# Two transformer blocks on one core: later convolutions in the projection stage, one product moved to GpSimd, and a new order of small steps

## The reference

```python
gu, gv, q, k, v, gate, b_logit, a_logit = split_cols(h @ w_in, IN_SIZES)
y_a = chunk_spatial_gating(gu, gv, ...)
qkv = silu(causal_dwconv(concatenate([q, k, v]), dn_conv))      # 4 taps along the tokens
q, k = l2norm(q), l2norm(k)
lmask = exp(where(tri, decay[..., :, None] - decay[..., None, :], -inf))
m = where(strict, einsum('bhnid,bhnjd->bhnij', k_beta, k) * lmask, 0)
sol = triangular_solve(m + eye, [v_beta, k_beta * exp(decay)])
qk = where(tri, einsum('bhnid,bhnjd->bhnij', q, k) * lmask, 0)
q_dec = q * exp(decay)                                          # the product that changes its engine
# recurrence over the chunks of tokens, with S the state of a head:
v_new = u_i - w_i @ S;  o = q_dec_i @ S + qk_i @ v_new;  S = S * cd_i + k_dec_i^T @ v_new
o = rmsnorm(o, dn_onorm) * silu(gate)
x = x + concatenate([y_a, o]) @ w_out
```

## Time and profile before

| what | value |
|---|---|
| median of 3 runs | 1570.03 us (1566.84 to 1570.04) |
| the profiled execution | 1569.95 us |
| its span, first to last instruction | 1568.2 us |
| mean granted TensorE clock in it | 0.993 |
| TensorE busy | 1543.0 us, 98% |
| VectorE busy | 878.0 us, 56% |
| ScalarE busy | 601.8 us, 38% |
| GpSimd busy | 104.9 us, 7% |

### The profile page before, as it was taken

One profiled execution on the slowest core, in us unless ns is written; L12 is line 12 of the kernel. 1 busy time (PEld: TensorE's weight loads), 2 busy tenths in 40 slices (PEclk: granted clock), 3 DMA queues, 4 the chain that ended last, 5 costly groups with the idle time before them and its releaser, 6 DMA issues.

```text
span 1568.2 us, 20461 instructions
## 1 busy us (share of the span) xinstructions
PE 1543.0 (98%) x8150; PEld 1275.4 (81%) x8150; DVE 878.0 (56%) x1331; ACT 601.8 (38%) x975; POOL 104.9 (7%) x91
## 2 busy tenths in 40 slices
PE   9898999999999999999999999999999999999998
PEld 7687789888788888888888877877888888888887
DVE  7676666654364344445565777644555663564465
ACT  6534333533344132322446344432334331332233
POOL 0000111220030000000040010100002000000000
PEclk9998999999999999999999999999999999999999
DMA  7211113531132322232332223221332233222221
GB/s 265 68 55 41 55 55 109 188 107 59 36 113 90 107 90 99 94 104 78 108 108 81 81 81 108 74 94 62 107 113 89 95 107 102 87 99 102 95 71 64
DMA packets 44941, 146.70 MB, mean 94 GB/s; under 512 B 5040, under 2 KB 8368, under 8 KB 44720
## 3 DMA queue, kind: packets, MB, share of 16 engines
q1 hardware_dynamic: 42448, 141.80, 26.8%
q10 hardware_dynamic: 2400, 3.61, 0.7%
HBM read 143.29 MB, written 2.10 MB: 93 GB/s over the span
## 4 chain that ended last, share of the span: by engine, by line
PE 87%; DVE 6%; ACT 4%; issue 3%; DMA 1%; POOL 0%; SPq 0%; DVEq 0%; POOLq 0%; ACTq 0%
PE bank L1308 26%; PE bank L1310 26%; PE bank L1309 26%; DVE w_lo L1884 1%; PE bank L1526 1%; PE bank L1543 1%; ACT w_hi L1604 1%; DVE temp L1876 1%; PE bank L1437 1%; PE bank L1465 1%; DVE temp L1869 1%; PE bank L1470 1%; PE bank L1273 0%; PE bank L1275 0%; PE bank L1274 0%
## 5 line engine op out<-in xcount | busy, mean ns | idle before, releaser
L1308 PE MATMUL bank<-a_hi,w_hi 128*128 128x512 f32 (+1 forms) x1275 | 499.3, 392 | 6.0 <-DVE gate L1869 6.0
L1310 PE MATMUL bank<-a_hi,w_lo 128*128 128x512 f32 (+1 forms) x1275 | 491.3, 385 | 0.0
L1309 PE MATMUL bank<-a_lo,w_hi 128*128 128x512 f32 (+1 forms) x1275 | 491.2, 385 | 0.0
L1884 DVE TENSOR_TENSOR w_lo<-w_raw,w_hi 128x1024 fp32r<-128x1024 f32 (+2 forms) x259 | 330.3, 1276 | 171.4 <-ACT w_hi L1604 171.0
L1604 ACT ACTIVATE w_hi<-w_raw 128x1024 fp32r<-128x1024 f32 (+2 forms) x259 | 267.0, 1034 | 198.3 <-PE bank L1310 195.0
L1308 PEld LDWEIGHTS bank<-a_hi,w_hi 128*128 128x128 f32 x1275 | 240.6, 189 | 57.5 <-issue 9.9
L1310 PEld LDWEIGHTS bank<-a_hi,w_lo 128*128 128x128 f32 x1275 | 240.4, 189 | 48.5
L1309 PEld LDWEIGHTS bank<-a_lo,w_hi 128*128 128x128 f32 x1275 | 240.9, 189 | 45.6
L1308 PE MATMUL bank<-b_hi,w_hi 128*128 128x512 f32 (+1 forms) x720 | 276.7, 384 | 0.4 <-ACT b_hi L1744 0.4
L1309 PE MATMUL bank<-b_lo,w_hi 128*128 128x512 f32 (+1 forms) x720 | 275.1, 382 | 0.0
L1310 PE MATMUL bank<-b_hi,w_lo 128*128 128x512 f32 (+1 forms) x720 | 275.1, 382 | 0.0
(11 more groups left out here) (317 smaller groups left out, 1196.2 us busy)
## 6 DMA issues: line engine op xcount, KB each, us to landing
w_raw<-weights_in SPq DMA_DIRECT2D x247, 512.0 KB, 3.2
w_raw<-weights_in SPq DMA_DIRECT2D x8, 384.0 KB, 2.9
x_first<-x_in SPq DMA_DIRECT2D x8, 256.0 KB, 5.8
xs<-x_in ACTq DMA_DIRECT2D x8, 256.0 KB, 5.0
w_raw<-weights_in SPq DMA_DIRECT2D x8, 256.0 KB, 2.7
mem_x<-mem_in SPq DMA_DIRECT2D x1, 1024.0 KB, 7.7
out<-xs SPq DMA_DIRECT2D x8, 128.0 KB, 1.8
w_raw<-front_in SPq DMA_DIRECT2D x5, 192.0 KB, 6.1
```

What stands on the lines that cost most here:

```text
L1308: pe.matmul(to, weights_hi[:, at], hi, start=k == k0, stop=False)
L1309: pe.matmul(to, weights_hi[:, at], lo, start=False, stop=False)
L1310: t = pe.matmul(to, weights_lo[:, at], hi, start=False, stop=k == k1 - 1)
L1884: dve.tensor_tensor(lo[:, 0:size], raw[:, n % SLOTS, 0:size], hi[:, 0:size].bitcast(F32), ALU.subtract).then_inc(split_dve.handle, 1)
```

## The change: what it does

- `halves_and_aside` and `conv_qkv`: the convolution of a projection is issued before the second half of the next one, and its SiLU ("shape") before the first half of the one behind that. Before, the convolution stood ahead of the next projection's first half and the SiLU behind that half.
- `split_ahead` gets a limit: one split at most per half projection.
- The sums of k stand one half projection later (an empty entry is put in between), and so do the norms behind them; the first spatial "mix" likewise.
- A gate's SiLU is an entry of its own ("silu"), apart from taking the projection out of its bank. Gates 0 and 1 are taken out of their banks right behind "decays"; before, this was done behind the halves of the next projection.
- In the opening, the second k-tile of `qkv1` stands ahead of sums 4, "norms" of head 0 and its "strict" stand ahead of "sums 0", so head 0 is one half projection further in its steps.
- "strict": the product of the queries with their decay moves from VectorE (line 2059) to GpSimd.
- k2, q2: "root A_SECOND" stands behind the first half of k2, "root A_TWICE" behind its second half, and q2 is issued whole behind both.
- `LAST_TILES`: pieces of 1, 2, 3 and 2 tiles in place of 3, 3 and 2.

```diff
-LAST_TILES = [slice(0, 3), slice(3, 6), slice(6, KT)]
+LAST_TILES = [slice(0, 1), slice(1, 3), slice(3, 6), slice(6, KT)]
...
-    def split_ahead(j):
-        while split[0] < min(j + LEAD + 1, N_LOADS) and (split[0] < SLOTS or split[0] - SLOTS in done or (
-                split[0] >= FIRST_EXTRA and PROJ["gate2", F2T - 1, 0] in done)):
-            add("split", split[0])
-            split[0] += 1
+    def split_ahead(j, most=SLOTS):
+        for _ in range(most):
+            if split[0] < min(j + LEAD + 1, N_LOADS) and (split[0] < SLOTS or split[0] - SLOTS in done or (
+                    split[0] >= FIRST_EXTRA and PROJ["gate2", F2T - 1, 0] in done)):
+                add("split", split[0])
+                split[0] += 1
...
     def halves_and_aside(name, n):
-        project(name, n, kb=KT // 2)
         while convolved:
             add("shape", convolved.pop(0))
+        project(name, n, kb=KT // 2, most=1)
         if aside:
             aside.pop(0)()
         yield
-        project(name, n, ka=KT // 2)
+        while projected:
+            add("conv", projected[0])
+            convolved.append(projected.pop(0))
+        project(name, n, ka=KT // 2, most=1)
         if aside:
             aside.pop(0)()
 
     def conv_qkv(n):
         if PROJ["qkv", n, 0] not in done:
             yield from halves_and_aside("qkv", n)
+        projected.append(n)
         yield
-        add("conv", n)
-        convolved.append(n)
...
-            aside.extend([lambda h=h: add("sums", h), lambda h=h: add("sums", H + h), lambda h=h: scaled(h)])
+            aside.append(lambda h=h: add("sums", h))
+            aside.extend([lambda: None, lambda h=h: add("sums", H + h), lambda h=h: scaled(h)])
             yield from conv_qkv(2 * H + h)
             for n in GATES_BEHIND.get(h, ()):
                 yield from halves_and_aside("gate", n)
                 add("gate", n)
+                add("silu", n)
                 yield
...
-                    aside.extend([lambda n=n: add("statistics", n), lambda n=n: add("normalise", n), lambda n=n: add("mix", n)])
+                    aside.extend([lambda n=n: add("statistics", n), lambda n=n: add("normalise", n)])
+                    if n == 0:
+                        aside.append(lambda: None)
+                    aside.append(lambda n=n: add("mix", n))
...
-    add("mm", (ahead, 0, 1))
+    add("mm", (ahead, 0, 2))
     add("sums", H)
     add("decays")
-    add("mm", (ahead, 1, KT - 2))
+    for n in GATES_BEHIND[0]:
+        add("gate", n)
+    add("mm", (ahead, 2, 5))
     first = delta_head(0)
     next(first)
-    add("mm", (ahead, KT - 2, KT))
+    add("mm", (ahead, 5, KT))
     done.add(ahead)
+    scaled(0)
+    next(first)
     add("sums", 0)
-    scaled(0)
     add("shape", 2 * H)
+    for n in GATES_BEHIND[0]:
+        add("silu", n)
     filler = itertools.chain(projections(), first_memory_keys())
-    aside.extend([lambda: add("gate", 0), lambda: add("gate", 1)])
...
-    project("k2", 0)
+    project("k2", 0, kb=KT // 2)
     add("root", A_SECOND)
-    project("q2", 0, kb=KT // 2)
+    project("k2", 0, ka=KT // 2)
     add("root", A_TWICE)
-    project("q2", 0, ka=KT // 2)
+    project("q2", 0)
     add("row", A_SECOND)
...
-                    qh = chunked(qkv[:, n, :])
-                    q.wait_ge(*sums_pe.at(n))
-                    q.wait_ge(*decay_act.at(n, 1))
-                    dve.tensor_tensor(qh, qh, chunked(temp("cum", n)), ALU.mult).then_inc(strict_dve.handle, 1)
...
+                elif kind == "strict":
+                    qh = qkv[:, n, :]
+                    q.wait_ge(*strict_pe.at(n))
+                    q.wait_ge(*sums_pe.at(n))
+                    q.wait_ge(*decay_act.at(n, 1))
+                    pool.tensor_tensor(qh, qh, temp("cum", n), ALU.mult).then_inc(strict_pool.handle, 1)
```

More of the change, by code:

```diff
@@ L197, in add, with project @@
         out.append((kind, n))
-    def split_ahead(j):
-        while split[0] < min(j + LEAD + 1, N_LOADS) and (split[0] < SLOTS or split[0] - SLOTS in done or (
-                split[0] >= FIRST_EXTRA and PROJ["gate2", F2T - 1, 0] in done)):
-            add("split", split[0])
-            split[0] += 1
-    def project(name, n, k0=0, ka=None, kb=None):
+    def split_ahead(j, most=SLOTS):
[4 more added lines that the diff above has]
+                split[0] += 1
+    def project(name, n, k0=0, ka=None, kb=None, most=SLOTS):
         j = PROJ[name, n, k0]
@@ L210, in project @@
             return
-        split_ahead(j)
+        split_ahead(j, most)
         add("mm", (j, ka, kb))
@@ L218, in first_split @@
         split[0] = j + 1
-    aside, convolved, normed_heads = [], [], []
+    aside, projected, convolved, normed_heads = [], [], [], []
     def halves_and_aside(name, n):
-        project(name, n, kb=KT // 2)
         while convolved:
             add("shape", convolved.pop(0))
+        project(name, n, kb=KT // 2, most=1)
         if aside:
@@ L275, in projections @@
         add("gate", H - 1)
+        add("silu", H - 1)
         yield
@@ L1004, in build_program @@
         mix_pe, mix_dve = signal("mix_pe", "mix"), signal("mix_dve", "mix", 2)
-        gate_dve, gate_act = signal("gate_dve", "gate"), signal("gate_act", "gate")
+        gate_dve, gate_act = signal("gate_dve", "gate"), signal("gate_act", "silu")
         decay_pe, decay_act, decay_dve = signal("decay_pe", "decay"), signal("decay_act", "decay", 2), signal("decay_dve", "decay", 2)
-        strict_pe, strict_dve = signal("strict_pe", "strict"), signal("strict_dve", "strict", 9)
+        strict_pe, strict_dve = signal("strict_pe", "strict"), signal("strict_dve", "strict", 8)
+        strict_pool = signal("strict_pool", "strict")
         turn_pe, turn_dve = signal("turn_pe", "turn"), signal("turn_dve", "turn")
@@ L1165, in temp_free @@
             return {"buf": lambda: conv_dve.at(i), "acc": lambda: shape_act.at(i, 1), "logits": lambda: rates_pe.at(),
-                    "v": lambda: statistics_pe.at(i), "normed": lambda: mix_dve.at(i), "cum": lambda: strict_dve.at(i),
+                    "v": lambda: statistics_pe.at(i), "normed": lambda: mix_dve.at(i), "cum": lambda: strict_pool.at(i),
                     "mem_sum": lambda: root_pe.at(A_MEMORY), "out": lambda: out_pe.at(i),
@@ L1499, in tensor_program @@
                             q.wait_ge(*strict_dve.at(h))
+                            q.wait_ge(*strict_pool.at(h))
                             q.wait_ge(*level_y_dve.at((h, LEVELS - 1)))
@@ L1704, in scalar_program @@
                     act.activation(temp("v", n), temp("v", n), ACT.Gelu_apprx_tanh).then_inc(spatial_v_act.handle, 1)
-                elif kind == "gate":
+                elif kind == "silu":
                     q.wait_ge(*gate_dve.at(n))
```

## The result

The changed kernel takes 1577.95 us (median of 4 runs, 1575.48 to 1578.5) against 1569.55 us of before on the same chip (4 runs, 1566.84 to 1570.04). The ratio is 1.0054, 95% interval 1.0041 to 1.0066: slower by 8.5 us, 6.4 to 10.4. I had forecast 1566.5 and a range up to 1571.5. The profiled execution took 1578.5 us, with a span of 1576.7, 8.5 above before's, so profile and medians tell of the same loss.

The account below looks back on a forecast made before the run. TensorE, busy 98%, bounds the kernel; only its waits and low clock can change. From 1569.95 us, stage -5.8, GpSimd product +0.1, middle +2.7 and end -0.3 give 1566.6, stated as 1566.5, range 1561 to 1571.5.

Parts of the forecast that it names:

- Gate 0's wait goes: Projection stage: TensorE's 6.0 us wait for VectorE to empty gate 0's bank and the low clock behind go, 7.3 us.
- The new waits up to 155 us: Projection stage: waits the hand walk of the new order expected, longest 3.1 us at sums 3 behind decay 2's chain.
- The stage wins 20.0 - 14.2 = 5.8: Projection stage: old waits and clock, 20.0 us, crossed out; the walk's new waits and clock cost 14.2; 5.8 us won.
- The clock: Projection stage: low clock behind new waits, including 1.7 us behind sums 3 and 1.4 behind level 1 of head 2.
- The product on GpSimd at nothing: Strict in four heads: GpSimd's duration is hidden; blocking of VectorE taken as 0.1 us for all four.
- rival D: Split or level mask behind strict: GpSimd blocks VectorE up to 1.4 us per head, 5.6 in all; 1572.1 us; chance 0.05.
- The middle, +2.7: k2, q2: root waits 2.5 us for GpSimd's last addition, 1.0 ahead of the row goes, clock 1.2: +2.7 us.
- The end, -0.3: Last tiles: first of four pieces leaves some 0.6 us sooner, moving 128 KB into idle DMA time: -0.3 us.
- C: Projection stage: gain given back as 0.4 us for eight convolutions nearer their SiLUs and sums, 3.2; 1569.7 us; chance 0.2.
- E: Low clock follows each added wait over 1 us, projection stage and root: 3.9 us more; 1570.4 us; chance 0.1.
- B: Projection stage: large wait at sums 3 or level 1 of head 2 doesn't appear: 1561.2 or 1563.2 us; chance 0.2.
- F: Middle: the sum comes sooner, so the moved root does what it seems meant to: 1563.9 us; chance 0.03.

Follow-up runs that it names:

- e5: Kernel before with only gates 0 and 1 taken out right behind the decays, their SiLUs separate entries in the old place: 1564.15 us, -4.9 against before.
- e3: Changed kernel with convolutions, their SiLUs, sums of k and first mix back in their old places: 1565.65 us, -4.1 against before.
- e12: e3 with the norms of heads 1 to 3 half a projection later, shifting heads 1 and 3: 1577.94 us, +7.8 against before.
- e11: Changed kernel with only the convolutions back early; SiLUs, sums, norms and first mix stay late: 1576.49 us, +7.8 against before.
- e8: Changed kernel with head 0 back to its old pace in the opening, gates still early: 1578.65 us, +9.7 against before.
- e1: Kernel before with only the middle changed (k2, q2 and their two roots): 1572.15 us, +3.0 against before.
- e4: Changed kernel with the product of queries and decay back on VectorE: 1578.38 us, +9.7 against before.
- e6: Changed kernel with mix 0 ahead of strict 3 again and five memory stage steps behind gate3's second half: 1575.92 us, +7.2 against before.
- e7: Changed kernel with sums 3, sums 7 and the norms of head 3 half a projection later: 1573.66 us, +5.8 against before.
- e10: e5 with the four last pieces, and sums 7 and the norms of head 3 half a projection later: 1562.13 us, -7.1 against before.
- e13: e10 with mix_bias moved ahead of gu0's first half: 1564.76 us, -4.5 against before.

## Why the prediction was wrong, step by step

- **Gate 0's wait goes**: right. It isn't there after, and alone it is worth 4.9 us (e5), not 7.3: 1.2 of the 6.0 net are waits again elsewhere, and the clock's share varies.
- **The new waits up to 155 us**: right, nearly row by row. The turn's copy 0.58 (0.65), sums 1 0.74 (0.5), strict 1 1.43 (1.5), level 4 of head 0 1.48 (1.1), sums 3 3.40 (3.1, and 0.5 at strict 2, which didn't come), sums 7 1.26 (0.85), mix_bias 1.61 (1.9), decay 0 none (0.2): 10.5 us of idle time against 10.3.
- **"The stage wins 20.0 - 14.2 = 5.8"**: this is the step that failed, and in it the list of new waits. "Head 3 is half a projection later" was priced at its last step alone, 0.8 at state 0 (measured 0.89). Of the same shift I had overlooked statistics 1 (2.19), level_y and solve behind normalise (0.87 and 0.33) and level_y(3,5) behind eight stage steps (2.08), 5.5 us, and the 1.6 of low clock behind the first. The walk assigned nothing to any step between 155 us and state 0. Not all of it is that shift's: behind 155 us e3, without it, waits 3.9 us in three (before: 1.8 in two), e12, with it, 7.7 in five, and the change 6.4 in five. Which step waits also depends on its neighbours: the change waits at statistics 1, e12, with the early mix, at strict 3. e12 shows that the shift of heads 1 and 3 brings such waits by itself, with the convolutions in their old places, and a loss as large as the whole change's; e11 and e8 show that neither the convolutions' place nor the opening decides it alone. Late sums bring late norms with them, since the norms are made from the sums; late SiLUs and a late first mix without late norms weren't run.
- **The clock**: I took 3.1 us for the new waits, and 6.3 were lost in the profiled execution, 2.9 of it behind sums 3 alone, where I had 1.7. I had read before's loss of 150 to 200 us as that of several waits; it lies behind one, of 1.66 us (last section), so a wait much shorter than 2.8 could cost as much.
- Forecast waits and clock, 14.2, and measured ones, 16.9 + 6.3 = 23.2, differ by 9.0; the start of state 0 differs from the forecast by 5.7 + 5.8 = 11.5. The last 2.5 us are in neither idle time nor clock. 0.7 of them lie ahead of the stage (the row of "rates" above). Some 1.7 stay: from that row to state 0, less idle time and clock, the two traces have 202.7 and 204.4 us of work. That each wait costs something beyond itself, when TensorE starts again, would be a guess, and the number of waits doesn't bear it out: the change has 12 over 0.3 us in place of 8, but e1, also with 8, has 203.0, and e3, with 7, has 203.6. Open.
- **The product on GpSimd at nothing**: right for the time (e4). The block that rival D spoke of does occur, in one of the change's four products. It was issued at 179.41, while VectorE's split of 179.24 to 180.53 ran, and took 2.27 us, to 181.68. The row of 181.12 above, both of whose inputs lie in SBUF, then took 1.11 us, and in e4, without the product on GpSimd, the same instruction took 0.68. The two rows between them, with one input in PSUM, took 0.41 as in e4. So the forecast's reason, three products from PSUM beside GpSimd's start, isn't what stood there; the price is small because it came once and was 0.4 us on VectorE. In e3 the taps that ran beside a product took 3.24 in place of 2.33. The rows, of the change, of e4, and of e3 (VectorE, GpSimd):

```profile
179.41 2.27 POOL L2384 TENSOR_TENSOR qkv<-qkv,temp 128x512 f32<-128x512 f32 x1
```

```profile
178.82 0.68 DVE L2055 TENSOR_TENSOR decays_t<-decays_t,small 128x512 f32<-128x512 f32 x1
```

```profile
128.90 3.24 DVE L1885 SCALAR_TENSOR_TENSOR temp<-temp,columns 128x512 f32<-128x512 f32 x3 [0.84 <-ACT temp L1676]
```

```profile
129.91 1.67 POOL L2378 TENSOR_TENSOR qkv<-qkv,temp 128x512 f32<-128x512 f32 x1 [24.64 <-PE bank L1420]
```

  The Trainium skill, "SBUF — State Buffer", Who interferes with whom, says that such a pair excludes each other and the second to issue waits. The traces agree: in the change the GpSimd product took 1.0 us longer than the 1.29 of an undisturbed one, where 1.1 us of the split were left when it was issued, and VectorE's product 0.4 longer, where 0.6 of GpSimd's were left. The price in the kernel's time was nothing that e4 could measure.
- **The middle, +2.7**: right, +3.0, by the mechanism named. **The end, -0.3**: -0.2 in the profile, too small for the medians.
- **The rivals**: C (many small coins) comes nearest, since the idle time is spread over twelve waits. But it was priced at 3.2 us in all and for convolutions too near their sums, and neither holds. E (more low clock) was near in size and wrong in place: the stage lost 3.2 us more to the clock than forecast, E had 3.9, but behind sums 3 and statistics 1 and not behind strict 1 and level 4, and it leaves over 8 of the 11.5 us unexplained. B, D and F are out.

## What to carry to other kernels

A written-out order of several interleaved chains is priced over its whole length, for each chain that the edit shifts, up to the point where the orders meet again; the first part walked is no sample of the rest. A chain moved by half a period against its neighbours changes who is next to whom on each engine and which buffer of a ring each step gets, and repairing one clash there made another in e6, e7, e8, e10 and e13. Take the part whose gain has a named wait and which keeps all other order (e5: -4.9 us) and measure it alone before the rest is built on it.

## What the runs showed of the hardware

The same wait costs low clock in one execution and none in another. Strict 2's wait of 2.8 us in before and in e1, with the same order ahead of it, ends at 137.44 in the one and at 140.08 in the other. The 7 us around and behind its end have a mean clock of 0.76 in before and of 1.00 in e1, so half speed, 1.2 GHz, for a part of that stretch or not at all. First the row of before, then that of e1:

```profile
137.00:144.00 7.00, 6.56 (x32) 5.84 (x33) 4.80 (x13) 0.30 (x3) 1.01 (x1) 0.76 0.01 2
```

```profile
140.00:147.00 7.00, 6.92 (x48) 6.00 (x48) 6.07 (x15) 0.51 (x1) 1.01 (x1) 1.00 0.01 2
```

The wait of 1.66 that ends at 151.93 in before is followed by 6 us at half speed, the row below; in e1 the same wait is followed by a clock of 1.00 (153 to 159 us). The root's 2.35 us are followed by 0.76 over 7 us in e1 (813 to 820) and by 1.00 in e3.

```profile
152.00:158.00 6.00, 6.00 (x28) 4.82 (x29) 3.72 (x9) 1.57 (x2) 0.00 (x0) 0.50 0.12 38
```

So a wait of 1.7 to 3.4 us had here a price between its own length and that plus some 3 us of clock, and a forecast should carry both.
